# Cached scores of a hybrid decoder step: products on 64 rows by 32 columns, memory and small-branch scores in a PSUM bank of their own, and cache copies issued at other places

## Chip, cores and metric

The kernel runs on one core of one Trainium2 chip. The metric is the device time of one execution in microseconds, as a median of runs. All matrix data are float32.

## What is computed

One decoder layer serves 256 prompt tokens and, beside them, 8 sequences with 4 new tokens each ("sample" tokens, 32 in all) that have a past of 2,048 tokens. One projection gives queries, keys and values of three attention branches and gates; then come the branches, a merge, an output projection, and a mixture of 32 experts of which each token uses 4. The part that the change touches is the attention of the sample tokens over the cached keys:

```python
idx_a = la + jnp.arange(n_new)[:, None] - jnp.arange(SWA_WINDOW)[None, :]
oa, _ = gathered_attention(qa, ka_ext, va_ext, idx_a, sink)          # branch A: last 128, 2 kv heads, 8 query heads
ob = dilated_sample(qb, kb_ext, vb_ext, lb)                          # branch B: 4 kv heads, three dilations
oc = memory_attention(qc, cache_mem_k[l], cache_mem_v[l])            # branch C: 256 memory tokens, 4 heads
...
swa_k_s.append(ka_ext[:, n_new:])                                    # caches moved on by the 4 new rows
dil_k_s.append(kb_ext[:, n_new:])
```

The last two lines (and their like for the values) are pure copies: the dilated caches are 8 x 2 MB of keys and 8 x 2 MB of values that go from HBM to HBM.

## The kernel before

The program is written engine by engine, with semaphores and an order set out by hand. Its stages for this case:

- **Projection, 0 to 100 us.** Weight blocks of 512 columns (2 MB; block 4 only 256 columns) alternate between two buffers, `load_wblk(i)`. SP asks for block i when TensorE is done with block i - 2. Block 5 holds the memory weights, blocks 6 to 11 the gate weights, 12 and 13 the branch weights.
- **Prompt attention with gate products in between, 100 to 204 us** (`score_products` at L1238, `gate_products` at L1192).
- **Cached scores, 204 to 256 us.** For each cached sequence b, `load_cache(b)` brings some 1.2 MB of keys in six transfers; TensorE transposes them in 19 pieces (`k_transposes`, L1340), VectorE and ScalarE evict them to `kTs` (L466, L926), and TensorE multiplies the queries with them (L1356). The order on TensorE is transposes of b + 1, then scores of b. Three key buffers exist: the load of cache i waits for the transposes of cache i - 3. The query operand `qw` is zero outside the four columns of sequence b, which ScalarE fills (`window_queries`, L890), so that all eight sequences add up into the same PSUM rows.
- **Softmax of these scores under gate products, then values, 256 to 303 us** (VectorE L1977 to L1998; `PR_B`, `PR_C`, `PR_A` are the three branches in SBUF; L1422 and L1430 the value products).
- **Branch and output projections, routing, experts, 303 us to the end.** SP streams 2 MB pieces of the experts' weights through nine buffers (`load_pair`, L611).

In the scores each matmul contracts over all 128 rows and writes 32 PSUM rows. Head h = 2m + r has its queries in the 64 rows of half r of `qw[:, r]`; the other half of the rows is zero. Heads 0 to 3 go to the four groups of 32 columns of the array. The small branch A has 2 x 4 products of 128 columns, kept in two planes v. PSUM banks 0 to 3 hold, by columns, `SC_B` (0 to 1247), `SC_C` (1248 to 1503, bank 2) and `SC_A` (bank 3, with new keys).

SP's queue is one order of transfers. `copy_cache()` issues the next of the 16 copies. Before, one stands behind each of the weight blocks 2 to 8, then come the key loads 0 and 1, the stores of the new keys and values, three copies, block 9 with two copies, block 10 with two copies, block 11, key load 2, two small copies of the branch A caches (L589), and the other loads; two copies remain and stand behind the first two pieces of the experts' weights (309 us).

Of the kernel before, what the change touches and what calls it, by code (L numbers as in the profile page):

```python
# [16 lines left out]
ALU = mybir.AluOpType  # L17
# [35 lines left out]
def constants():  # L53

    cols, at = [], {}

    def put(name, a):
        a = np.asarray(a, np.float32).reshape(P, -1)
        at[name] = (sum(c.shape[1] for c in cols), a.shape[1])
        cols.append(a)  # L60

    p = np.arange(P)
    put("ident", np.eye(P))
    put("tri", (p[:, None] < p[None, :]))
# [12 lines left out]
    put("mask_b", np.stack([np.where((dist >= 0) & (dist <= w) & (dist % d == 0), 0, NEG)  # L77
                            for w, d in GROUPS], 1))

    b, i = p // NQ_S % NB_S, p % NQ_S  # L80
    new_b, new_i = np.arange(NS) // NQ_S, np.arange(NS) % NQ_S
    same = b[:, None] == new_b
    before = new_i <= i[:, None]
    itself = new_i == i[:, None]
    put("smask_a", np.where(np.concatenate([np.arange(LA) > i[:, None], same & before], 1), 0, NEG))
    recent = 1536 + np.arange(512)
    far = np.arange(384) // 4 * 16 + np.arange(384) % 4
    near = 1536 + np.arange(128) // 4 * 16 + np.arange(128) % 4
    q = PAST + i[:, None]
    put("smask_b", np.where(np.concatenate([  # L90
        ((q - recent) % 4 == 0) & (q - recent <= 512),
        ((q - np.concatenate([far, near])) % 16 == 0) & (q - np.concatenate([far, near]) <= 2048),
        q - recent[384:] <= 128,
        same & before, same & itself, same & itself], 1), 0, NEG))
    half = HD // 8
    inv = np.float32(500000.0) ** (-np.arange(half, dtype=np.float32) / np.float32(half))
    pos = np.stack([p, P + p, PAST + p % NQ_S], 1).astype(np.float32)
    ang = (pos[:, :, None] * inv.astype(np.float32)).astype(np.float32)
    put("cos", np.cos(ang))
    put("sin", np.sin(ang))  # L100

    row_h, row_b, row_i, tile = p % 32 // 8, p % 8 // 4, p % 4, p // 32
    put("omask_bc", (row_h[:, None, None] == np.arange(4)) & (row_b[:, None, None] == np.arange(2)[:, None]))
    put("omask_a", (row_b == tile // 2)[:, None] & ((tile % 2)[:, None] == np.arange(2)))
    put("osel", np.arange(NS) == (8 * np.arange(4)[:, None] + 4 * row_b[:, None, None] + row_i[:, None, None]))
    put("orow", np.concatenate([row_h[:, None] == np.arange(4), (tile < 3)[:, None], (tile == 3)[:, None]], 1))
    return np.ascontiguousarray(np.concatenate(cols, 1)), at

def lay_params(gain_rows, sinks, b_router, w_router):  # L110

    return np.ascontiguousarray(np.concatenate([
        gain_rows.reshape(3, KC, P).transpose(2, 0, 1).reshape(P, 3 * KC),
        np.broadcast_to(sinks.reshape(1, 8), (P, 8)),
        np.repeat(sinks.reshape(2, 4).T, NS, 0),
        np.broadcast_to(b_router.reshape(1, NE), (P, NE)),
        w_router.reshape(KC, P, NE).transpose(1, 0, 2).reshape(P, KC * NE),
        gain_rows[2].reshape(4, P, 2).transpose(1, 0, 2).reshape(P, KC)], 1), dtype=np.float32)
# [7 lines left out]
def build(nc, d):  # L126
    es = ExitStack()
    with es:
# [29 lines left out]
        def const(name, n=P):  # L158
            a, w = CONST_AT[name]
            return cst[0:n, a:a + w]  # L160
# [72 lines left out]
        def bank(i, n=1):  # L233
            return ps[:, i * 512:(i + n) * 512]
# [121 lines left out]

        SP = bank(0, 4)
        SC_B = SP[:, 0:NSM_B]
        SC_C = SP[:, NSM_B:NSM_B + LM]
        SC_A = SP[:, 1536:1536 + 2 * NSM_A].rearrange("p (v n) -> p v n", n=NSM_A)  # L360
        PR_B = s_probs[:, 0:NSM_B]
        PR_C = s_probs[:, NSM_B:NSM_B + LM]
        PR_A = s_probs[:, NSM_B + LM:NSM_B + LM + 2 * NSM_A].rearrange("p (v n) -> p v n", n=NSM_A)
# [106 lines left out]
        def _(sp):  # L470
# [6 lines left out]
            def load_wblk(i):  # L477
# [11 lines left out]
                elif i in W_BR:  # L489
# [4 lines left out]
                    sp.dma_start(dst[:, 4:6, :], d["w_br_b"][0].rearrange("(m p) n -> p m n", p=P)[:, :, n]).then_inc(s, 16)  # L494
                    sp.dma_start(dst[:, 6:8, :], d["w_br_c"][0].rearrange("(m p) n -> p m n", p=P)[:, :, n]).then_inc(s, 16)

            copies = [(x, b) for x in ("k", "v") for b in range(NB_S)]

            def copy_cache():
# [67 lines left out]
            sp.dma_start(cst[:, P:], d["consts"][:, P:]).then_inc(S["cst_in"], 16)  # L567
            for i in range(1, 9):
                load_wblk(i)
                if i >= 2:  # L570
                    copy_cache()
            sp.wait_ge(S["tr_evicted"], TR_H + TR_Q)
            load_cache(0)
            load_cache(1)
            store_new_kv()
            copy_cache()
            copy_cache()
            copy_cache()
            for i in (9, 10):
                load_wblk(i)  # L580
                copy_cache()
                copy_cache()
            load_wblk(11)
            load_cache(2)
# [4 lines left out]
                sp.dma_start(dst.rearrange("b (a n) -> b a n", a=16), src.rearrange("b (a n) -> b a n", a=16)) \  # L589
                    .then_inc(S["copy_dma"], 16)  # L590

            for i in range(3, 12):
                load_cache(i)
            load_wblk(12)
            for i in range(12, 16):
# [490 lines left out]
        def _(pe):  # L1086
# [257 lines left out]
            for b in range(NB_S):  # L1344
                if b + 1 < NB_S:
                    k_transposes(b + 1)
                kTs = kTs2[b % 2]
                done = 5 * (b + 1)
                pe.wait_ge(S["ktv_evicted"], (done + 1) // 2)
                pe.wait_ge(S["kta_evicted"], done // 2)  # L1350
                pe.wait_ge(S["qw_ready"], b + 1)
                win = slice(28 - 4 * b, 60 - 4 * b)
                first, last = b == 0, b == NB_S - 1

                def add(out, lhs, rhs, start):
                    return pe.matmul(out, lhs, rhs, start=start, stop=last, skip_group_check=True)  # L1356

                for part in range(5):
                    for h in range(4):
                        m, r = h // 2, h % 2  # L1360
                        row = slice(32 * h, 32 * h + 32)
                        kb = kTs[:, m * 1024:m * 1024 + 896]
                        q = qw[:, r]
                        if part == 0:
                            add(SP[row, 0:512], q[:, 6 + m, win], kb[:, 0:512], first)
                        elif part == 1:
                            add(SP[row, 512:896], q[:, 8 + m, win], kb[:, 512:896], first)
                        elif part == 2:
                            add(SP[row, 896:1024], q[:, 8 + m, win],
                                kb[:, 0:512].rearrange("p (a s) -> p a s", s=16)[:, :, 0:4], False)  # L1370
                        elif part == 3:
                            add(SP[row, 1024:1152], q[:, 4 + m, win], kb[:, 384:512], first)
                        else:
                            add(SP[row, NSM_B:NSM_B + LM], q[:, 10 + m, win],
                                kTs[:, 1920 + m * LM:1920 + (m + 1) * LM], False)
                for v in range(2):
                    for j in range(4):
                        ins = add(SC_A[32 * j:32 * j + 32, v, 0:LA], qw[:, v, j, win], kTs[:, 896:1024],
                                  first and v == 0)
                ins.then_inc(S["s_scores_b"], 1)  # L1380

            for g in range(3):
                for h in range(4):
# [2 lines left out]
                              kT_v[:, 1 + m, SEQ:TT], start=False, stop=True, skip_group_check=True)  # L1386
            for v in range(2):
                for j in range(4):
                    ins = pe.matmul(SC_A[32 * j:32 * j + 32, v, LA:NSM_A], qn[:, v, j, :], kT_v[:, 0, SEQ:TT],
                                    start=False, stop=True, skip_group_check=True)  # L1390
            ins.then_inc(S["s_scores_done"], 1)

# [60 lines left out]
                              start=(g == 0), stop=False, skip_group_check=True)  # L1453
            for v in range(2):
                for j in range(4):
                    ins = pe.matmul(bank(4)[32 * j:32 * j + 32, 64 * v:64 * v + 64], pT_n[:, 1 + v, 32 * j:32 * j + 32],
                                    kv[0:NS, 2, 384 + 64 * v:448 + 64 * v], start=False, stop=True, skip_group_check=True)
            ins.then_inc(S["s_tok_done"], 1)
            pe.wait_ge(S["s_tokb_evicted"], 1)
# [367 lines left out]
        def _(v):  # L1827
# [147 lines left out]
            v.wait_ge(S["s_scores_done"], 1)  # L1975
            nb, ncc, na = s_st[:, 0:1], s_st[:, 1:2], s_st[:, 2:4]
            link(v.tensor_tensor(PR_B, SC_B, const("smask_b"), ALU.add))  # L1977
            v.tensor_tensor(PR_A, SC_A, const("smask_a").unsqueeze(1).to_broadcast([P, 2, NSM_A]), ALU.add)
            v.tensor_reduce(nb, PR_B, AX.X, ALU.max, negate=True)
            link(v.tensor_reduce(ncc, SC_C, AX.X, ALU.max, negate=True))  # L1980
            link(v.tensor_reduce(na, PR_A, AX.X, ALU.max))
# [425 lines left out]
```

## Time and profile before

| | |
|---|---|
| median of 3 runs | 1313.25 us (1311.59 to 1314.88) |
| profiled execution | 1311.65 us, span 1309.8 us |
| busy share | TensorE 94%, VectorE 31%, ScalarE 19%, GpSimd 3% |
| chain that ended last | TensorE 64%, DMA 31% |
| L1340 (transposes of keys) | 152 records, 204.5 to 249.0 us |
| L1356 (scores) | 448 records, 209.3 to 255.7 us |

### The profile page before, as it was taken

What the parts mean: (1) busy time and instruction counts of PE and PEld (TensorE: products, weight loads), DVE (VectorE), ACT (ScalarE), POOL (GpSimd) and SP (SyncE); (2) the same over time, 40 slices, a digit from 0 to 9 for tenths busy, and PEclk for the clock granted to TensorE, in tenths of its full rate; (3) what the DMA queues carried; (4) which work ended last, traced back from release to release, by engine and by line L of the source; (5) the groups of instructions that cost most, each with busy time, mean ns of one, the idle gap of its engine ahead of it and who ended that gap; (6) DMA issues with size and microseconds to landing.
All of it is one profiled execution on the core that took longest, in us unless ns stands there. A gap on an engine that the chain in (4) does not pass through costs nothing.

```text
span 1309.8 us, 15220 instructions
## 1 busy us (share of the span) xinstructions
PE 1236.6 (94%) x6387; PEld 530.0 (40%) x6402; DVE 400.8 (31%) x908; ACT 245.3 (19%) x487; POOL 34.7 (3%) x47
## 2 busy tenths in 40 slices
PE   9999997999999999999999999889999999999996
PEld 4456675667553333333333333223333333333332
DVE  2244452314444232142231314222231313222233
ACT  3212443213111211112011111101011111101012
POOL 0000005000020000000000000000000000000000
PEclk9999998999999999999999999999999999999999
DMA  8686999689989999999999999999999999999994
GB/s 303 239 315 231 339 369 288 192 256 353 364 312 393 409 427 428 427 426 428 427 428 427 428 428 427 428 426 428 427 428 427 427 428 427 426 428 427 429 426 194
DMA packets 71673, 499.19 MB, mean 381 GB/s; under 512 B 5952, under 2 KB 29120, under 8 KB 45984
## 3 DMA queue, kind: packets, MB, share of 16 engines
q1 hardware_dynamic: 70752, 495.80, 93.3%
q0 software_dynamic: 848, 2.36, 0.6%
q8 instruction: 53, 0.87, 0.3%
q14 instruction: 20, 0.16, 0.0%
HBM read 495.29 MB, written 36.96 MB: 406 GB/s over the span
## 4 chain that ended last, share of the span: by engine, by line
PE 64%; DMA 31%; DVE 2%; issue 1%; ACT 1%; SPq 0%; DVEq 0%; ACTq 0%
DMA ring<-in_w_gate_up 20%; PE ps L1724 18%; PE ps L1763 12%; DMA late<-in_w_gate_up 9%; PE ps L1192 7%; PE ps L1108 5%; PE ps L1680 3%; PE ps L1624 3%; PE ps L1474 2%; PE ps L1487 2%; PE ps L1356 1%; PE ps L1340 1%; PE ps L1741 1%; PE ps L1643 1%; PE ps L1170 1%; DMA cq<-in_cache_mem_k 1%
## 5 line engine op out<-in xcount | busy, mean ns | idle before, releaser
L1724 PE MATMUL ps<-ring,cq 128*64 128x512 f32 x1376 | 313.9, 599 | 27.6 <-DMA ring<-in_w_gate_up 27.6
L1724 PEld LDWEIGHTS ps<-ring,cq 128*64 128x64 f32 x1376 | 93.9, 137 | 220.0 <-issue 161.8
L1763 PE MATMUL ps<-ring,cq 128*64 128x512 f32 x656 | 148.8, 595 | 0.0
L992 ACT ACTIVATE cq<-ps 128x512 f32<-128x512 f32 x32 | 19.1, 597 | 456.6 <-PE ps L1741 456.6
L1192 PE MATMUL ps<-arena,ring 128*128 128x288 f32 x384 | 102.3, 412 | 2.0 <-ACT ring L836 2.0
L2230 DVE TENSOR_REDUCE stat<-ps 128x1 f32<-128x288 f32 x15 | 6.9, 457 | 290.0 <-PE ps L1656 290.0
L1724 PE MATMUL ps<-cq 128*64 128x512 f32 x336 | 77.0, 595 | 5.0 <-DMA cq<-in_w_gate_up 5.0
L1192 PEld LDWEIGHTS ps<-arena,ring 128*128 128x128 f32 x384 | 69.6, 189 | 25.6 <-issue 4.9
L1763 PEld LDWEIGHTS ps<-ring,cq 128*64 128x64 f32 x656 | 45.4, 136 | 80.9 <-issue 76.4
L1108 PE MATMUL ps<-ring,arena 128*128 128x512 f32 (+3 forms) x240 | 72.3, 555 | 0.9 <-DMA ring<-in_w_in 0.9
L2258 DVE TENSOR_TENSOR x_tok<-x_tok,ps 64x512 f32<-64x512 f32 (+2 forms) x51 | 43.9, 860 | 73.2 <-PE ps L1680 67.8
L1006 ACT ACTIVATE cq<-ps 64x512 f32<-64x512 f32 x32 | 18.8, 589 | 230.2 <-PE ps L1763 230.2
L1624 PE MATMUL ps<-h_tok,cq 128*64 128x512 f32 x248 | 60.0, 604 | 0.0
L2131 DVE TENSOR_TENSOR cq<-ps,params 128x512 f32<-128x512 f32 x31 | 21.3, 686 | 110.7 <-PE ps L1643 110.7
L1108 PEld LDWEIGHTS ps<-ring,arena 128*128 128x128 f32 (+1 forms) x240 | 31.8, 163 | 37.9 <-issue 34.9
L1724 PE MATMUL ps<-late,cq 128*64 128x512 f32 x176 | 41.2, 601 | 5.7 <-DMA late<-in_w_gate_up 5.7
L1724 PEld LDWEIGHTS ps<-cq 128*64 128x64 f32 x336 | 23.3, 136 | 49.5 <-issue 37.8
L1763 PE MATMUL ps<-arena,cq 128*64 128x512 f32 x176 | 39.7, 592 | 0.7 <-issue 0.7
L1763 PE MATMUL ps<-late,cq 128*64 128x512 f32 x176 | 40.2, 598 | 0.0
L1680 PE MATMUL ps<-late,cq 128*32 128x512 bf16 (+1 forms) x180 | 39.7, 378 | 0.0
L1724 PE MATMUL ps<-arena,cq 128*64 128x512 f32 x160 | 36.3, 596 | 3.1 <-DMA arena<-in_w_gate_up 3.1
L2143 DVE TENSOR_TENSOR cq<-cq,ps 128x512 f32<-128x512 f32 x32 | 22.0, 687 | 42.3 <-ACT ps L988 41.7
(371 smaller groups left out, 1211.0 us busy)
## 6 DMA issues: line engine op xcount, KB each, us to landing
ring<-in_w_gate_up SPq DMA_DIRECT2D x86, 2048.0 KB, 37.9
ring<-in_w_down SPq DMA_DIRECT2D x40, 2048.0 KB, 38.8
cq<-in_w_gate_up SPq DMA_DIRECT2D x20, 2048.0 KB, 38.6
late<-in_w_gate_up SPq DMA_DIRECT2D x11, 2048.0 KB, 37.1
arena<-in_w_down SPq DMA_DIRECT2D x11, 2048.0 KB, 40.3
arena<-in_w_gate_up SPq DMA_DIRECT2D x10, 2048.0 KB, 36.9
late<-in_w_down SPq DMA_DIRECT2D x10, 2048.0 KB, 38.8
ring<-in_w_in SPq DMA_DIRECT2D x9, 2048.0 KB, 12.0
```

The source lines that it names most:

```text
L992: act_e.activation(xTe if isinstance(b, int) and b == NE - 1 else aTe, bank(4)[:, :].rearrange("p (q m) -> p q m", m=P), ACT.Copy).then_in ...
L1108: ins = pe.matmul(bank((n % 2) * 3 + t)[k_rows(t, k), 0:b - a], hT_v[:, k, TOK0[t]:TOK0[t] + NTOK[t]], wblk[n % 2][:, k, 0:b - a], **k_gro ...
L1192: ins = pe.matmul(bank(gate_bank(m))[:, 0:TT], wblk[(6 + m // 4) % 2][:, k, (m % 4) * P:(m % 4 + 1) * P], hT_v[:, k, :], start=(k == 0), s ...
L1474: ins = pe.matmul(bank(3 * (dt % 2) + br)[:, 0:TT], wblk[blk % 2][:, k, (dt % 4) * P:(dt % 4 + 1) * P], oT[:, k, :], start=(k == ks[0]), s ...
L1487: ins = pe.matmul(bank(wout_bank[t][n])[k_rows(t, k), :], hT_v[:, k, TOK0[t]:TOK0[t] + NTOK[t]], wo[n][:, k, :], **k_group(t, k))
L1624: pe.matmul(bank(6)[64 * h:64 * h + 64, :], sel[:, t, :], h_row[t][:, h * 512:(h + 1) * 512], start=(t == 0), stop=False, skip_group_check ...
L1680: ins = pe.matmul(out, slot_hot[:, tok], y_part[i][:, 512 * h:512 * h + 512], start=(i == 0), stop=(i == 2), skip_group_check=True)
L1724: ins = pe.matmul(bank(gu0 + u)[64 * h:64 * h + 64, :], xTe[:, k % 4, (k // 4) * 64:(k // 4) * 64 + 64], pair_buf[slot][:, a:a + 512], sta ...
L1763: ins = pe.matmul(bank(7 if last else 5)[64 * h:64 * h + 64, :], aT[:, kk % 4, (kk // 4) * 64:(kk // 4) * 64 + 64], pair_buf[slot][:, a:a ...
L2131: v.tensor_tensor(xTe4, xps, gain_x, ALU.mult).then_inc(S["xt_ready"], 1)
L2143: v.tensor_tensor(act, u_clip, bank(gu0), ALU.mult).then_inc(S["act_ready"], 1)
L2258: v.tensor_tensor(xs, xs, rows, ALU.add).then_inc(S["sc_added"], 1)
```

## The change

The scores' products contract over 64 rows instead of 128: each takes the row half r in which its head's queries lie. The dilated products of head h keep column group h. The products of memory and of branch A ("crossed") use the same row half and the other column group of the pair m, so they lie on parts of the array that the dilated products leave out. They are issued between the dilated ones, and they write bank 3 alone; the new keys of branch A go to bank 2. Masks, sinks and selectors are laid out for the new rows, and one mask addition on VectorE becomes two. In SP's queue the copies are issued by a table: 2, 2, 2, 1, 1, 3, 1 behind the weight blocks 2 to 8, none behind the stores of the new keys, one each behind blocks 9 and 10, one behind key load 7, and one remains for 309 us.

```diff
+            COPIES_BEHIND = (0, 0, 2, 2, 2, 1, 1, 3, 1, 1, 1)
             for i in range(1, 9):
                 load_wblk(i)
-                if i >= 2:
+                for _ in range(COPIES_BEHIND[i]):
                     copy_cache()
...
             store_new_kv()
-            copy_cache()
-            copy_cache()
-            copy_cache()
             for i in (9, 10):
                 load_wblk(i)
-                copy_cache()
                 copy_cache()
             load_wblk(11)
             load_cache(2)
...
-            for i in range(3, 12):
+            for i in range(3, 8):
+                load_cache(i)
+            copy_cache()
+            for i in range(8, 12):
                 load_cache(i)
...
-        SC_C = SP[:, NSM_B:NSM_B + LM]
-        SC_A = SP[:, 1536:1536 + 2 * NSM_A].rearrange("p (v n) -> p v n", n=NSM_A)
+        SC_C = SP[:, 1536:1536 + LM]
+        SC_A = SP[:, 1536 + LM:2048].rearrange("p (s n) -> p s n", n=LA)
+        SN_A = SP[:, NSM_B:NSM_B + 2 * NS].rearrange("p (s n) -> p s n", n=NS)
...
-                for part in range(5):
+                def add(out, r, chunk, rhs, start):
+                    half = slice(64 * r, 64 * r + 64)
+                    return pe.matmul(out, qw[half, r, chunk, win], rhs[half], start=start, stop=last, skip_group_check=True)
+
+                def crossed(part, h):
+                    m, r = h // 2, h % 2
+                    row = slice(32 * (2 * m + 1 - r), 32 * (2 * m + 1 - r) + 32)
+                    if part == 0:
+                        return add(SC_C[row, :], r, 10 + m, kTs[:, 1920 + m * LM:1920 + (m + 1) * LM], first)
+                    return add(SC_A[row, part - 1, :], r, 2 * m + part - 1, kTs[:, 896:1024], False)
+
+                for part in range(4):
                     for h in range(4):
...
                         if part == 0:
-                            add(SP[row, 0:512], q[:, 6 + m, win], kb[:, 0:512], first)
+                            own = add(SP[row, 0:512], r, 6 + m, kb[:, 0:512], first)
+                            crossed(0, h)
                         elif part == 1:
-                            add(SP[row, 512:896], q[:, 8 + m, win], kb[:, 512:896], first)
+                            crossed(1, h)
+                            own = add(SP[row, 512:896], r, 8 + m, kb[:, 512:896], first)
+                            crossed(2, h)
                         elif part == 2:
-                            add(SP[row, 896:1024], q[:, 8 + m, win],
-                                kb[:, 0:512].rearrange("p (a s) -> p a s", s=16)[:, :, 0:4], False)
-                        elif part == 3:
-                            add(SP[row, 1024:1152], q[:, 4 + m, win], kb[:, 384:512], first)
+                            own = add(SP[row, 896:1024], r, 8 + m,
+                                      kb[:, 0:512].rearrange("p (a s) -> p a s", s=16)[:, :, 0:4], False)
                         else:
-                            add(SP[row, NSM_B:NSM_B + LM], q[:, 10 + m, win],
-                                kTs[:, 1920 + m * LM:1920 + (m + 1) * LM], False)
-                for v in range(2):
-                    for j in range(4):
-                        ins = add(SC_A[32 * j:32 * j + 32, v, 0:LA], qw[:, v, j, win], kTs[:, 896:1024],
-                                  first and v == 0)
-                ins.then_inc(S["s_scores_b"], 1)
+                            own = add(SP[row, 1024:1152], r, 4 + m, kb[:, 384:512], first)
+                own.then_inc(S["s_scores_b"], 1)
...
-            v.tensor_tensor(PR_A, SC_A, const("smask_a").unsqueeze(1).to_broadcast([P, 2, NSM_A]), ALU.add)
+            mask_a = const("smask_a").unsqueeze(1)
+            v.tensor_tensor(PR_A[:, :, 0:LA], SC_A, mask_a[:, :, 0:LA].to_broadcast([P, 2, LA]), ALU.add)
+            v.tensor_tensor(PR_A[:, :, LA:], SN_A, mask_a[:, :, LA:].to_broadcast([P, 2, NS]), ALU.add)
```

The other edits of the diff (constants `omask_bc`, `omask_a`, `orow`, the sinks in `lay_params`, the row group g in the products of new keys and new values) move rows and add no instruction.

## Rows read from the trace of the kernel before

**Rows 1.** Windows: stretch; busy of PE, PEld, DVE, ACT, POOL; clock, DMA share, GB/s
```profile
222.98:230.78 7.80, 7.80 (x76) 5.65 (x77) 1.25 (x2) 1.79 (x3) 6.03 (x9) 0.66 0.96 273
...
378.40:1309.80 931.40, 874.10 (x4098) 299.57 (x4113) 258.85 (x573) 140.79 (x237) 0.00 (x0) 0.99 0.99 417
```

**Rows 2.** Chain that ended last, in order of time: start us, us, what
```profile
204.50 2.45 PE ps L1340 x19
...
222.98 4.32 PE ps L1340 x19
227.30 3.48 PE ps L1356 x56
...
241.50 2.37 PE ps L1340 x19
243.87 2.95 PE ps L1356 x56
...
249.28 2.99 PE ps L1356 x56
252.55 0.25 ACT ring L890
252.93 3.00 PE ps L1356 x54
256.33 11.87 PE ps L1192 x48
```

**Rows 3.** Waits, 200 to 262 us: who waited for what, total, times, longest
```profile
PE ps L1340 <- DMA cq<-in_cache_mem_k: 4.4, 1, 4.4
...
PE ps L1340 <- DMA ring<-in_cache_mem_k: 0.9, 1, 0.9
```

**Rows 4.** The same chain, 64-row products of the prompt's scores, two row halves
```profile
161.52 1.50 PE ps L1238 x12
```

**Rows 5.** Timeline: memory weights' first product, last softmax step; in brackets idle before
```profile
86.65 1.55 PE L1170 MATMUL ps<-ring 128*128 128x512 f32 x3 [0.60 <-DMA ring<-in_w_mem_kv]
...
266.61 0.48 DVE L1998 TENSOR_TENSOR ring<-ring,stat 128x320 f32<-128x320 f32 x1
```

**Rows 6.** Windows of the DMA engines, columns as in the first group
```profile
42.80:56.00 13.20, 13.20 (x31) 5.92 (x32) 2.73 (x4) 3.86 (x6) 0.00 (x0) 1.00 0.81 317
73.00:77.00 4.00, 4.00 (x22) 1.09 (x20) 0.00 (x0) 0.84 (x2) 0.00 (x0) 1.00 0.00 0
195.00:207.00 12.00, 10.35 (x86) 8.47 (x84) 2.57 (x4) 5.45 (x10) 2.96 (x6) 1.00 0.86 299
...
356.00:372.00 16.00, 16.00 (x102) 11.37 (x100) 8.96 (x28) 2.86 (x5) 7.33 (x5) 1.00 0.65 209
```

**Rows 7.** Timeline of SP's queue: start, us until the last is issued
```profile
77.03 0.37 SPq L485 DMA_DIRECT2D ring<-in_w_mem_kv  x1
...
123.43 0.37 SPq L488 DMA_DIRECT2D ring<-in_w_in  x1
...
151.58 11.29 SPq L506 DMA_DIRECT2D out_dil_v_s<-in_cache_dil_v  x2
...
196.33 6.25 SPq L531 DMA_DIRECT2D ring<-in_cache_dil_k  x3
...
206.97 0.37 SPq L528 DMA_DIRECT2D cq<-in_cache_dil_k  x1
```

**Rows 8.** DMA issues at 42, 76, 207, 227 us: KB, us to landing
```profile
ring<-in_w_in SPq DMA_DIRECT2D x1, 2048.0 KB, 7.8
...
ring<-in_w_mem_kv SPq DMA_DIRECT2D x1, 2048.0 KB, 9.6
...
cq<-in_cache_mem_k SPq DMA_DIRECT2D x1, 256.0 KB, 13.0
...
cq<-in_cache_mem_k SPq DMA_DIRECT2D x1, 256.0 KB, 4.1
```

**Rows 9.** Timeline of TensorE, value products of cache 0 and the first of cache 1
```profile
274.34 0.42 PE L1422 MATMUL ps<-cq,late 128*32 128x256 f32 x3 [0.72 <-ACT late L945]
...
275.67 0.41 PE L1422 MATMUL ps<-cq,late 128*32 128x256 f32 x2
```

More of the change, by code:

```diff
@@ L102, in constants @@
     row_h, row_b, row_i, tile = p % 32 // 8, p % 8 // 4, p % 4, p // 32
-    put("omask_bc", (row_h[:, None, None] == np.arange(4)) & (row_b[:, None, None] == np.arange(2)[:, None]))
-    put("omask_a", (row_b == tile // 2)[:, None] & ((tile % 2)[:, None] == np.arange(2)))
+    put("omask_bc", ((row_h ^ (tile == 3))[:, None, None] == np.arange(4)) & (row_b[:, None, None] == np.arange(2)[:, None]))
+    put("omask_a", (row_b == tile // 2)[:, None] & ((1 - row_h % 2)[:, None] == np.arange(2)))
     put("osel", np.arange(NS) == (8 * np.arange(4)[:, None] + 4 * row_b[:, None, None] + row_i[:, None, None]))
-    put("orow", np.concatenate([row_h[:, None] == np.arange(4), (tile < 3)[:, None], (tile == 3)[:, None]], 1))
+    put("orow", np.concatenate([(2 * (row_h // 2) + tile % 2)[:, None] == np.arange(4), (tile < 3)[:, None], (tile == 3)[:, None]], 1))
     return np.ascontiguousarray(np.concatenate(cols, 1)), at
@@ L114, in lay_params @@
         np.broadcast_to(sinks.reshape(1, 8), (P, 8)),
-        np.repeat(sinks.reshape(2, 4).T, NS, 0),
+        np.repeat(np.stack([sinks.reshape(2, 4)[1 - g % 2, 2 * (g // 2):2 * (g // 2) + 2] for g in range(4)]), NS, 0),
         np.broadcast_to(b_router.reshape(1, NE), (P, NE)),
@@ L1353, in _ @@
                 first, last = b == 0, b == NB_S - 1
-                def add(out, lhs, rhs, start):
-                    return pe.matmul(out, lhs, rhs, start=start, stop=last, skip_group_check=True)
-                for part in range(5):
+                def add(out, r, chunk, rhs, start):
[8 more added lines that the diff above has]
+                for part in range(4):
                     for h in range(4):
@@ L1362, in _ @@
                         kb = kTs[:, m * 1024:m * 1024 + 896]
-                        q = qw[:, r]
                         if part == 0:
-                            add(SP[row, 0:512], q[:, 6 + m, win], kb[:, 0:512], first)
+                            own = add(SP[row, 0:512], r, 6 + m, kb[:, 0:512], first)
+                            crossed(0, h)
                         elif part == 1:
-                            add(SP[row, 512:896], q[:, 8 + m, win], kb[:, 512:896], first)
+                            crossed(1, h)
+                            own = add(SP[row, 512:896], r, 8 + m, kb[:, 512:896], first)
+                            crossed(2, h)
                         elif part == 2:
-                            add(SP[row, 896:1024], q[:, 8 + m, win],
-                                kb[:, 0:512].rearrange("p (a s) -> p a s", s=16)[:, :, 0:4], False)
-                        elif part == 3:
-                            add(SP[row, 1024:1152], q[:, 4 + m, win], kb[:, 384:512], first)
-                        else:
-                            add(SP[row, NSM_B:NSM_B + LM], q[:, 10 + m, win],
-                                kTs[:, 1920 + m * LM:1920 + (m + 1) * LM], False)
-                for v in range(2):
-                    for j in range(4):
-                        ins = add(SC_A[32 * j:32 * j + 32, v, 0:LA], qw[:, v, j, win], kTs[:, 896:1024],
-                                  first and v == 0)
-                ins.then_inc(S["s_scores_b"], 1)
+                            own = add(SP[row, 896:1024], r, 8 + m,
+                                      kb[:, 0:512].rearrange("p (a s) -> p a s", s=16)[:, :, 0:4], False)
+                        else:
+                            own = add(SP[row, 1024:1152], r, 4 + m, kb[:, 384:512], first)
+                own.then_inc(S["s_scores_b"], 1)
             for g in range(3):
@@ L1388, in _ @@
                 for j in range(4):
-                    ins = pe.matmul(SC_A[32 * j:32 * j + 32, v, LA:NSM_A], qn[:, v, j, :], kT_v[:, 0, SEQ:TT],
+                    g = 2 * (j // 2) + 1 - v
+                    ins = pe.matmul(SN_A[32 * g:32 * g + 32, j % 2, :], qn[:, v, j, :], kT_v[:, 0, SEQ:TT],
                                     start=False, stop=True, skip_group_check=True)
@@ L1455, in _ @@
                 for j in range(4):
-                    ins = pe.matmul(bank(4)[32 * j:32 * j + 32, 64 * v:64 * v + 64], pT_n[:, 1 + v, 32 * j:32 * j + 32],
+                    g = 2 * (j // 2) + 1 - v
+                    ins = pe.matmul(bank(4)[32 * j:32 * j + 32, 64 * v:64 * v + 64], pT_n[:, 1 + j % 2, 32 * g:32 * g + 32],
                                     kv[0:NS, 2, 384 + 64 * v:448 + 64 * v], start=False, stop=True, skip_group_check=True)
```

## The prediction

> **What bounds the kernel now.** I read the page's chain first, then the windows, the chain in order of time, the waits and the DMA views of 195 to 256 us. From 378 us on the experts' weights keep the DMA engines full (share 0.99 for 931 us) [rows 1]; this stretch starts when the work before it ends, so what is saved ahead of it moves the end by as much. Before 378 us TensorE works almost without a pause, except where the cached scores are made, from 204.5 us (end of the wait for L883) to the first gate product at 256.33. Its chain is: transposes of a cache (T, L1340), scores of the cache before (S, L1356), eight of each. Undisturbed T takes 2.37 to 2.45 us (2.42) and S 2.95. Eight of each are 43.0 us, 0.66 goes to the wait for the last query window (252.27 to 252.93), 0.40 to the new keys behind the last S, so 44.1 [rows 2]. The stage lasts 51.8. The rest is waiting for keys: 0.9 for cache 2, 4.4 for cache 3 [rows 3]; after that the granted clock of the stretch is 0.66 [rows 1], so the engine fell to its 1.2 GHz level for part of it, and T and S beside it take 4.32 and 3.48 [rows 2], 1.9 and 0.5 above the later ones. Together 7.7 us lost to late keys. So two terms are in reach: 8 S, and 7.7.
>
> **Change, part 1: the scores.** A float32 matmul is two records here. 48 records of 288 columns take 11.87 us [rows 2]: 0.86 ns a column and record, 1.72 ns a column of a matmul. Before, each of four column groups takes 512 + 384 + 128 + 128 (dilated) + 256 (memory) + 2 x 128 (small branch) = 1,664 columns: 2.86 us, against 2.95 measured, so the four groups do run beside each other and almost nothing else counts. The diff contracts over 64 rows, not 128, and puts memory and small branch on the other row half in the other column group of the pair. Still 28 matmuls, 56 records; a group's dilated products are 1,152 columns, 1.98 us, and its 512 others should run beside them. That two row halves overlap the trace shows at L1238: six matmuls of 64 rows and 256 columns would be 2.64 us in a line and 1.32 in two, and take 1.50 [rows 4]. That is 0.18 above the columns. No row shows two row halves together with four column groups. Bounds for S: 1.98 below, 2.95 above where the halves don't overlap (the same columns in a line), exclusion is a rival. I take 1.98 + 0.18, and 0.04 for eight streams to start instead of two, 2.2, by the L1238 row, which is the same kind of pair. Saved: 8 x 0.75 = 6.0 us (bounds 7.8 and 0).
>
> Can the transposes keep pace? The evictions of T end during the S behind it: with 0.69 us each on VectorE the last ends about 0.7 us after T, still inside 2.2. The 0.66 for the last window stays.
>
> On VectorE the mask add of 128x320 (0.48 us at that size) becomes two, 128x256 and 128x64: an estimate of 0.15 us more, the fixed part of one such step, from the same size at L1998. The last normalising step ends at 267.09 and TensorE comes out of its gate products at 268.20 [rows 2, 5]: slack of about 1 us, so nothing; without that cover 0.15. The new keys keep 40 records; masks, sinks and selectors change only in values.
>
> **Change, part 2: the copies.** 16 copies of 2 MB, HBM to HBM, stand in SP's queue. Before, 7 are issued behind weight blocks 2 to 8, 3 behind the stores of new keys, 4 behind blocks 9 and 10, 2 at 309 us. After: 12 behind blocks 2 to 8 (2, 2, 2, 1, 1, 3, 1), 2 behind 9 and 10, 1 behind key load 7, 1 at 309. A load with a copy moved 13.2 us x 317 GB/s = 4.2 MB in the stretch 42.8 to 56 with a share of 0.81, so 10.7 us for both; 5.3 for a copy.
>
> Early on this is hidden. The engines are empty at 73 to 77 (share 0.00) [rows 6]. Load 2 with two copies is 16 us from 28, to 44; load 3 the same to about 60, its block landed long before that (7.8 us with a copy behind it [rows 8]); block 4 is half as large, with two copies to about 75.5; the memory weights are asked for at 77.03. They already come 0.6 us late (9.6 us from issue, TensorE free at 86.05) [rows 5, 7, 8], so a copy still moving there counts at once: 0 taken, bounds 0 and 2. Behind block 7, from 101 us, load and three copies are 21 us, and block 8 is asked for at 123.43 [rows 7]. SP's own issues (0.6 us each, 11.3 for two where the ring is full [rows 7]) delay only SP waits that are for TensorE anyway.
>
> Between 144 and 195 us five copies fewer, 26 us of transfers: no wait for a transfer stands there, so nothing there, but the backlog at 195 goes. Of 26.9 MB issued from 123 to 195 windows of 2 us show 25.8 moved, so about 1.1 MB was left, 3 to 4 us at the 299 GB/s of 195 to 207 [rows 6]. And SP was held 6.25 us in issuing load 2's far keys [rows 7]. A cache is 1.25 MB, 4.6 us at the 273 GB/s that the engines give while they carry keys (share 0.96) [rows 1]. After: block 11 (5 us), keys 2 (4.6), the small copies (2.5), biases (1.5) from 196.5 on end at 210; keys 3, asked for at 206.97, at 214.7 by bytes alone, against 222.9 (its last piece took 13.0 us; unloaded 4.1 [rows 8]). The faster TensorE now wants them at 204.5 + 3 x 2.42 + 2 x 2.2 = 216.1. Then it wants one cache every 4.6 us, which is what a cache takes. So keys and TensorE bound the stage about equally up to cache 7, and the copy behind load 7 (about 227 us) runs against that load's own last pieces. I leave 1.5 us of stalls and a full clock: 7.7 - 1.5 = 6.2 saved (bounds 7.7 and, if keys 3 to 7 land no earlier, about 0 with half of term 1 lost too).
>
> The copy taken from 309: share 0.65 at 356 to 372 [rows 6], the engines idle because all nine weight buffers are full; nothing, bound 5.3.
>
> **Sum.** 6.0 + 6.2 = 12.2 us, the stage ends at 244.1. Profiled: 1311.65 us (span 1309.8) to 1299.4. The median is 1313.25, 1.6 above that execution: 1301.0.
>
> **Rivals.**
> 1. Keys still decide. If keys 3 land at 223 as before, T of cache 3 starts there and its slow clock stays; only the five S behind it gain, 3.8 to 4.5: 1309. For it: the chain's 13 us for one 256 KB piece, three loads in flight, which get in each other's way. Against: 1.1 MB less ahead of them, and SP not held at 196.
> 2. Issue order costs. At L1422/L1430 the products of the next cache start at 275.67 on column groups whose own four records, 0.22 apart from 274.34, ended at about 275.2 [rows 9]: a full group holds up the others. If each group holds only one matmul ahead, the crossed 128-column ones, issued before the own ones, push heads 2 and 3 back by 0.2 to 0.4 us: S 2.5, 2.4 us less gain: 1303.5.
> 3. The row halves run no closer than before: S 2.95, only 6.2: 1307.
> 4. Slower: the two row halves exclude each other while four column groups are in use, at the own products of heads 0 and 1, which write one PSUM bank from different halves. Heads alternate between the halves in the program, so each waits for the last: 4 x 1.98 = 7.9 us, the stage ends at 204.5 + 19.4 + 1.1 + 8 x 7.9 = 288.2, 31.9 later: 1345. It decides from S = 3.9 us, where the stage ends at 256.3 again. Against: L1238 shows halves overlapping, though in different banks.
> 5. A copy makes the memory weights late, 2 to 5 us: 1304 to 1306.
> 6. The copy taken from 309 helps after all, up to 5.3: 1296.
>
> Beside rival 4, the Trainium skill, TensorEngine Tiling (Array Packing), Gotcha 1, says that different row tiles can't write one PSUM bank at the same time; the diff gives a bank of its own only to memory and small branch. No row here shows that case. By that rule it would be the exclusion; heads 0 and 1 write different partitions, which is why I hold it small.
>
> Beside rival 2, the Trainium skill, TensorE: Matmul & The Clock Gate, step-by-step part, says that matmuls stay in program order and only weight loads are pulled ahead. By that rule, taken strictly, S before would be about 5.7 us (each of 6,656 columns for one record); by that rule the trace does not agree, with 2.95.
>
> **How the numbers follow.** Forecast 0.60; rival 1 0.12; 2 0.10; 3 0.06; 4 0.04; 5 0.04; 6 0.04. Range 1296.5 to 1308.5: both terms at their best (15.5 us, 1297.7) and the spread of the three runs below, rivals 2, 3 and 5 above; half of rival 1 and all of 4 stay out. The forecast's own range is 1298 to 1303. A measurement tells about 0.3%, 3.9 us, from no change. Faster 0.87 (all but 4 and part of 1), same 0.09, slower 0.04.
>
> **What would show it.** S at L1356 near 2.2 us (forms of 64 rows), first gate product behind it near 244; no wait above 2 us for keys 2 or 3 and a granted clock of 1.00 throughout 204 to 244; the wait for memory weights at 86 us still 0.6; DMA share near 1 from 196 to 235; the stretch from 378 us (then 366) as long as before, 931. Wrong if S is above 2.6, if T of cache 3 starts after 219, if the copy behind load 7 makes cache 7 late by more than 2 us, or if the last stretch changes its length.

## The result, and the profile after

The changed kernel takes 1303.62 us (median of 6 runs, 1302.45 to 1306.16), the kernel before 1312.26 us in the 6 runs beside it: ratio 0.9935, 95% interval 0.9924 to 0.9945, 8.6 us faster. The forecast was 1301.0 in a range of 1296.5 to 1308.5. Two more sets on other occasions gave 1301.53 against 1312.53 (0.9928, 0.9903 to 0.9953) and 1303.80 against 1311.87 (0.9934, 0.9921 to 0.9948): 11.0 and 8.1 us faster. The profiled execution took 1302.55 us with a span of 1300.7.

The chain that ended last, in order of time, answers to [rows 2] (start us, us, what; L1341 are the transposes, L1358 the scores, L1193 the gate products):

```profile
78.82 10.54 DMA ring<-in_w_mem_kv
89.41 14.00 PE ps L1171 x32
...
207.26 2.45 PE ps L1341 x19
...
212.71 6.43 DMA cq<-in_cache_mem_k
219.18 2.53 PE ps L1341 x19
221.71 2.52 PE ps L1358 x40
224.23 2.37 PE ps L1341 x19
226.60 2.29 PE ps L1358 x40
228.89 2.46 PE ps L1341 x19
231.35 2.29 PE ps L1358 x40
...
243.81 2.33 PE ps L1358 x40
...
246.68 11.87 PE ps L1193 x48
```

From the first transposes to the first gate product the stage is 246.68 - 207.26 = 39.4 us, against 51.8. S is 2.29 us instead of 2.95 (the chain counts 40 of its 56 records, the timeline has all). The chain still passes through the transfer of keys 3 (L1341 at 219.18), but this is no wait any more: its last piece lands 6.4 us after issue, not 13.0 [rows 8], hardly later than TensorE gets there. The waits of TensorE up to 262 us, against [rows 3]:

```profile
PE ps L1109 <- DMA ring<-in_w_in: 2.2, 2, 1.5
...
PE ps L1171 <- DMA ring<-in_w_mem_kv: 1.6, 1, 1.6
...
PE ps L1358 <- ACT ring L891: 0.7, 1, 0.7
```

No wait for keys is among the eight largest (the smallest of those is 0.5 us); of the loads, only those of the first weight block and the memory weights are left, and both are longer than before (0.9 and 0.6 then). The windows (stretch; busy of PE, PEld, DVE, ACT, POOL; clock, DMA share, GB/s), against [rows 1]:

```profile
207.26:246.68 39.42, 38.65 (x641) 31.24 (x641) 13.29 (x20) 14.91 (x34) 21.08 (x30) 1.00 1.02 328
246.68:1300.70 1054.02, 999.18 (x4894) 380.07 (x4893) 310.32 (x705) 166.66 (x289) 9.32 (x9) 0.99 0.97 402
```

In the stage the clock is 1.00 and the DMA engines are full at the same time (1.02): both bounds are met at once. The stretch behind it is 1054.0 us, 0.5 longer than before (1309.8 - 256.33 = 1053.5). The 12.4 us of the stage shrink to 9.1 in the span because this execution was late on the way: the piece of the first weight block that SP asks for at 3.1 us landed at 13.06 us instead of 11.27, ahead of the first copy (1.8 us), the memory weights took 1.0 us more from issue to landing than before, and 0.5 us came in behind the stage. So everything between 89 and 207 us stands 2.76 us later than before.

### The profile page after: what moved, and what is told of

Read it like the earlier page. It is cut to its first block, busy times and chain, and to the rows that moved or that the text cites. A ratio compares the mean times of both kernels' runs of the same rounds, so it can differ in the third digit from the quotient of the medians.

```text
span 1300.7 us, 15236 instructions
## 1 busy us (share of the span) xinstructions
PE 1234.3 (95%) x6402; PEld 530.1 (41%) x6402; DVE 403.4 (31%) x909; ACT 245.3 (19%) x487; POOL 34.7 (3%) x47
## 4 chain that ended last, share of the span: by engine, by line
PE 60%; DMA 36%; DVE 2%; ACT 1%; issue 1%; SPq 0%; DVEq 0%; ACTq 0%
DMA ring<-in_w_gate_up 19%; PE ps L1730 17%; PE ps L1769 11%; DMA cq<-in_w_gate_up 9%; PE ps L1193 7%; PE ps L1109 5%; DMA late<-in_w_gate_up 3%; DMA ring<-in_w_down 3%; PE ps L1630 3%; PE ps L1480 2%; PE ps L1493 2%; PE ps L1341 1%; PE ps L1649 1%; PE ps L1686 1%; PE ps L1358 1%; PE ps L1171 1%
## 5 line engine op out<-in xcount | busy, mean ns | idle before, releaser
L1193 PE MATMUL ps<-arena,ring 128*128 128x288 f32 x384 | 102.3, 412 | 2.1 <-ACT ring L837 2.1
L1193 PEld LDWEIGHTS ps<-arena,ring 128*128 128x128 f32 x384 | 69.6, 189 | 25.6 <-issue 4.9
L1007 ACT ACTIVATE cq<-ps 64x512 f32<-64x512 f32 x32 | 18.9, 591 | 230.5 <-PE ps L1769 230.5
L1769 PE MATMUL ps<-late,cq 128*64 128x512 f32 x176 | 40.2, 598 | 0.0
```

Of the source, the lines that this page charges most:

```text
L1193: ins = pe.matmul(bank(gate_bank(m))[:, 0:TT], wblk[(6 + m // 4) % 2][:, k, (m % 4) * P:(m % 4 + 1) * P], hT_v[:, k, :], start=(k == 0), s ...
L1769: ins = pe.matmul(bank(7 if last else 5)[64 * h:64 * h + 64, :], aT[:, kk % 4, (kk // 4) * 64:(kk // 4) * 64 + 64], pair_buf[slot][:, a:a ...
```

## The experiments

Stage below means the time from the first transposes of keys to the first gate product behind the scores, read from each chain. The profile of each is of one execution.

**The two parts by themselves.** `scores_only` keeps the new products and issues the copies at the old places; `copies_only` is the reverse.

```diff
 # scores_only, against the changed kernel
-            COPIES_BEHIND = (0, 0, 2, 2, 2, 1, 1, 3, 1, 1, 1)
+            COPIES_BEHIND = (0, 0, 1, 1, 1, 1, 1, 1, 1, 2, 2)
...
             store_new_kv()
+            copy_cache()
+            copy_cache()
+            copy_cache()
             for i in (9, 10):
                 load_wblk(i)
+                copy_cache()
                 copy_cache()
...
-            for i in range(3, 8):
-                load_cache(i)
-            copy_cache()
-            for i in range(8, 12):
+            for i in range(3, 12):
                 load_cache(i)
```

> The scores' products as changed, the copies at their old places. If late keys set the first half of the stage whatever the products take, S falls to 2.3 us, the transposes of cache 3 still begin some 18 us after those of cache 0, at a low clock after the wait, and only the five S behind them gain: 3.3 to 4 us, 1308 to 1309. If keys were late only because copies were ahead of them by chance and the shorter S counts eight times, 5.3 us: 1307. In both cases the wait for the memory weights stays 0.6.

> The copies at their new places, the scores' products as before. If the copies alone made the keys late, no wait above 1 us stands in the stage, the clock is 1.00 throughout, S stays 2.95 and the stage falls from 51.8 to 44.5; less 1.0 for memory weights that come later: 6.3 us, 1306. If the three loads in flight get in each other's way whatever is ahead, a wait of 3 us or more for keys 3 stays and the gain is under 3 us.

scores_only: 1308.01 us against 1312.53, ratio 0.9965 (0.9952 to 0.9977). Its chain:

```profile
203.81 2.45 PE ps L1342 x19
...
210.52 12.12 DMA cq<-in_cache_mem_k
222.68 3.72 PE ps L1342 x19
226.40 2.49 PE ps L1359 x40
228.89 2.37 PE ps L1342 x19
231.25 2.29 PE ps L1359 x40
```

Its waits for keys:

```profile
PE ps L1342 <- DMA cq<-in_cache_mem_k: 3.4, 1, 3.4
...
PE ps L1342 <- DMA ring<-in_cache_mem_k: 2.0, 1, 2.0
```

The last piece of keys 3 again takes 12.1 us, its transposes begin 18.9 us after those of cache 0 (18.5 before), and take 3.72 us: what the first scores save is waited away, and the stretch 216 to 228 has a clock of 0.84 here too. The stage is 251.24 - 203.81 = 47.4 us, 4.4 less than before: 0.4 above the first reading's 3.3 to 4, and short of the second's 5.3. The wait for the memory weights was 0.5 us.

copies_only: 1305.62 us, ratio 0.9956 (0.9938 to 0.9974). Its chain:

```profile
205.48 4.91 PE ps L1340 x38
210.40 2.95 PE ps L1356 x56
213.34 2.37 PE ps L1340 x19
215.71 2.95 PE ps L1356 x56
218.66 2.46 PE ps L1340 x19
...
249.61 11.87 PE ps L1192 x48
```

Transposes and scores follow each other without a gap: 44.1 us, 7.7 less, exactly what the late keys and the slow clock had cost. Here, too, three loads of keys are in flight, so it was the copies' places that made the keys late. The memory weights cost 0.1 us more than before (a wait of 0.7), not the 1.0 that was taken off, and the kernel gained 6.9 us, not 6.3. The two parts add up: 4.4 + 7.7 = 12.1, against 12.4, 11.7 and 11.7 in three executions of both (`changed_again` 245.54 - 205.46 = 40.1, `changed_third` 248.06 - 207.95 = 40.1). If the keys are already in time, the scores save 44.1 - 39.4 to 40.1, 4.0 to 4.7 us, of 5.3, since 0.6 to 1.3 us come back as waits.

**The changed kernel again, and the start.**

> The changed kernel once more beside the others: 8 to 9 us under the kernel before. If the 1.8 us by which its first weights came later is chance between executions, the start of the products of pair 4 to 5 of block 0 moves again, by a microsecond or so either way; if it belongs to the change, it stands near 13.1 us again and near 11.3 in the kernels with the old copies.

> The changed kernel on the same chip as the run before it: 8.5 to 11 us under the kernel before, the memory weights 1.6 to 2.1 us late, and 1 to 2 us above the kernel with the copies taken from behind blocks 3 and 4.

The gains of these two sets, 11.0 and 8.1 us, lie outside what was expected of them (8 to 9, and 8.5 to 11). The same piece of the first weight block landed at 10.74 and 11.88 us, against 13.06 in the first profile; the kernel before has 11.27, scores_only 10.69, copies_only 12.12. The start moves by up to 2.4 us between executions, of one kernel and from kernel to kernel, before anything of the change is issued; it is no effect of it. TensorE waited 2.1 and 1.8 us for the memory weights.

**Who makes the memory weights late.** `copy_off_block4` has the table 2, 2, 1, 1, 2, 3, 1 behind blocks 2 to 8, `mem_clear` 2, 1, 1, 1, 2, 3, 2, `mem_clear_309` 2, 1, 1, 1, 2, 3, 3 with none left for 309 us. Only the tuple differs from the changed kernel.

```diff
-            COPIES_BEHIND = (0, 0, 2, 2, 2, 1, 1, 3, 1, 1, 1)
+            COPIES_BEHIND = (0, 0, 2, 2, 1, 1, 2, 3, 1, 1, 1)    # copy_off_block4
+            COPIES_BEHIND = (0, 0, 2, 1, 1, 1, 2, 3, 2, 1, 1)    # mem_clear
+            COPIES_BEHIND = (0, 0, 2, 1, 1, 1, 2, 3, 3, 1, 1)    # mem_clear_309
```

> The changed kernel with one copy taken from behind block 4 and put behind block 6 (table 2, 2, 1, 1, 2, 3, 1). If the second copy behind block 4 makes the memory weights late, the engines are empty again just ahead of their issue, TensorE waits 0.6 us for them instead of 1.6, and the whole is 1 us faster than the changed kernel. If the later weights come from the later start of that execution, the wait stays at 1.6 and nothing moves.

> The changed kernel with table 2, 1, 1, 1, 2, 3, 2: one copy each behind blocks 3 and 4, as in the kernel before, two behind 6 and 8. The run with one copy off block 4 had empty engines ahead of the memory weights and TensorE still waited 1.6 us. If copies in the two blocks ahead make these weights late in some way other than a queue, the wait falls to 0.6 here and the kernel is 1 us faster than the changed one. If the 0.6 to 2.1 us are chance from one execution to the next, it lies anywhere between and the times are the same within 1 us.

> The table 2, 1, 1, 1, 2, 3, 3: one copy each behind blocks 3 and 4 and none left for 309 us. The wait for the memory weights is 0.6 us. If the experts' stream starts only when its nine buffers are full and the engines idle ahead of it, the stretch from the first gate product behind the scores to the end stays 1053.5 to 1055 us and the kernel is 1 to 2 us faster than the changed one, by the memory weights alone. If the copy at 309 us delays the stream, that stretch is up to 5 us shorter.

The wait, from the waits of copy_off_block4, and the engines ahead of the issue (columns as above):

```profile
PE ps L1171 <- DMA ring<-in_w_mem_kv: 1.6, 1, 1.6
```

```profile
72.00:78.00 6.00, 6.00 (x27) 2.03 (x25) 0.00 (x0) 0.84 (x2) 0.00 (x0) 1.00 0.03 11
```

With one copy off block 4 the engines are empty (share 0.03, 0.97 in the changed kernel), and the weights are as late as ever. The other way round, in copies_only the share ahead of the issue is 0.89 and the wait 0.7. The later start of the execution is not the reason either: changed_again started early (10.74 us) and waited 2.1, mem_clear late (12.48) and waited 0.6. With one copy each behind blocks 3 and 4, mem_clear has:

```profile
PE ps L1171 <- DMA ring<-in_w_mem_kv: 0.6, 1, 0.6
```

Over all kernels, one profile each: with one copy behind each of blocks 3 and 4, the wait was 0.6, 0.5, 0.6 and 0.5 (before, scores_only, mem_clear, mem_clear_309). With more it was 1.5 to 2.2 in eight executions and 0.7 in two (copies_only, copies_at_gates). copies_at_gates has the same copies as copy_off_block4 up to block 5, and waited 0.7 against 1.6, so chance between executions has a part. That the copies behind blocks 3 and 4 have another, of about 1 us, is what the fourteen waits suggest; it is not shown. A queue that hasn't drained at 78 us isn't the explanation, and how an earlier copy could delay a load when the engines have run empty in between stays open.

The late weights can cost more than their wait. In changed_third, copy_off_block4 and copies_at_stores (waits of 1.8, 1.6, 1.6 us) the 32 products behind them took 15.6 to 15.7 us instead of 14.0; in the other five executions with a wait of 1.5 us or more, changed_again among them, they took 14.0. Chain and windows 84 to 104 of changed_third:

```profile
88.48 15.63 PE ps L1171 x32
```

```profile
84.00:104.00 20.00, 18.19 (x59) 8.33 (x58) 11.53 (x41) 1.58 (x3) 0.00 (x0) 0.91 0.87 348
```

and of changed_again:

```profile
84.00:104.00 20.00, 17.93 (x68) 9.27 (x61) 12.90 (x44) 1.77 (x4) 0.00 (x0) 1.00 0.80 304
```

The granted clock fell in one and not in the other, though the other's wait was longer (2.1 us).

copy_off_block4 took 1301.03 us against 1312.53, ratio 0.9913 (0.9896 to 0.9930), the lowest of all the sets, although its profile has the late weights and the slow clock; that profile is of its slowest execution (1304.28, the others 1300.3 to 1301.2). mem_clear took 1301.58 us against 1311.03, ratio 0.9928 (0.9914 to 0.9942). mem_clear_309 took 1301.53 against 1311.87, 0.9922 (0.9909 to 0.9934), on the chip where changed_third took 1303.80, 0.9934. Both beat the kernel before; over the changed kernel the 2.3 us (1 to 2 were expected) are of the size that the wait and the clock explain, but the intervals overlap, and copy_off_block4 is as fast, so a gain from this is not shown. The stretch behind the stage was 1299.7 - 244.60 = 1055.1 us with no copy at 309 us, no shorter than with one: that copy delays nothing.

**Issue order, and what is beside what.** `crossed_last` issues the crossed products behind all dilated ones; `own_only` leaves out the crossed products of caches 1 to 7.

```diff
 # crossed_last: the calls of crossed() in the parts are gone, and instead
+                for part in range(3):
+                    for h in range(4):
+                        own = crossed(part, h)
                 own.then_inc(S["s_scores_b"], 1)
...
 # own_only, at each of the three calls
-                            crossed(0, h)
+                            if b == 0:
+                                crossed(0, h)
```

> The changed kernel with the crossed products issued behind all dilated ones of a cache, the same 28 matmuls. If a part of the array that holds four records holds up all that is issued behind it, the crossed ones start only when the last dilated ones are let in, at 1.5 to 1.6 us, and S is 2.6 to 2.7 us. If a part holds only two, 2.9 or more. If issue order doesn't matter, S stays 2.29.

> Leaves out the memory and small-branch scores of caches 1 to 7 (their softmax runs on the scores of cache 0 alone). What is left are 16 matmuls a cache, 1,152 columns in each column group. If the crossed products are fully beside the dilated ones, S falls only from 2.29 to some 2.15 us (1.98 of columns and 0.18), and the rest of the gap to 1.98 belongs to filling and draining. If the two row halves share something that slows both, S falls to 2.05 or less.

One T and S late in the stage, crossed_last:

```profile
238.10 2.46 PE ps L1341 x19
240.56 2.60 PE ps L1358 x48
```

and own_only:

```profile
235.09 2.08 PE ps L1358 x32
237.17 2.46 PE ps L1341 x19
```

crossed_last has S 2.56 to 2.63, 0.27 or more above the changed order, at or a little under the 2.6 to 2.7 of the reading with four records held for each part; so issue order counts, and the reading with two held (2.9 or more) doesn't fit. The weight loads of crossed_last agree (timeline of PEld, in brackets the idle time before): the dilated products have 32 of the 56; the first 20 come in fours and an eight, at the pace of the products, and the last 12 and all 24 crossed ones from 232.08 on.

```profile
230.55 0.15 PEld L1358 LDWEIGHTS ps<-ring 64*32 64x32 f32 x8 [0.17 <-issue]
231.01 0.13 PEld L1358 LDWEIGHTS ps<-ring 64*32 64x32 f32 x4 [0.30 <-issue]
231.44 0.13 PEld L1358 LDWEIGHTS ps<-ring 64*32 64x32 f32 x4 [0.30 <-issue]
231.76 0.13 PEld L1358 LDWEIGHTS ps<-ring 64*32 64x32 f32 x4 [0.20 <-issue]
232.08 0.83 PEld L1358 LDWEIGHTS ps<-ring 64*32 64x32 f32 x36 [0.20 <-issue]
```

In own_only S is 2.08: 1,152 columns at 1.72 ns are 1.98, and 0.10 is all that filling and draining add, as before the change (0.09). So the 512 crossed columns cost 0.21 us of the 0.88 that they would cost in line: three quarters of that time is hidden, not all. The value lies between the two that were expected, at 2.15 and at 2.05, so it doesn't tell whether the 0.21 is issue (twelve more matmuls between the starts of the dilated ones) or something that the halves share.

**Which copies hold up the keys.** Seven copies stand between 144 and 195 us before, two in the changed kernel. `copies_at_stores` has five there (three behind the stores, one each behind blocks 9 and 10, table 1, 2, 1, 1, 1, 2, 1 for blocks 2 to 8), `copies_at_gates` four (two each behind 9 and 10, table 2, 2, 1, 1, 1, 2, 1). `copy7_late` leaves the copy behind key load 7 to 309 us.

```diff
-            COPIES_BEHIND = (0, 0, 2, 2, 2, 1, 1, 3, 1, 1, 1)
+            COPIES_BEHIND = (0, 0, 1, 2, 1, 1, 1, 2, 1, 1, 1)    # copies_at_stores
...
             store_new_kv()
+            copy_cache()
+            copy_cache()
+            copy_cache()
...
+            COPIES_BEHIND = (0, 0, 2, 2, 1, 1, 1, 2, 1, 2, 2)    # copies_at_gates
...
                 load_wblk(i)
+                copy_cache()
                 copy_cache()
...
             for i in range(3, 8):                                # copy7_late
                 load_cache(i)
-            copy_cache()
```

> The changed kernel with three copies put back behind the stores of new keys (145 us), one behind each of blocks 9 and 10, and nine behind blocks 2 to 8. If only the backlog that is left at 195 us makes the keys late, the engines work these three off by 190, no wait above 1.5 us for keys stands in the stage, and it lasts 39.4 to 40.1 us as in the changed kernel. If the number of copies between 144 and 195 us counts, waits of 2 to 5 us come back.

> The changed kernel with two copies each behind blocks 9 and 10 as before, none behind the stores, ten behind blocks 2 to 8. If what is asked for last before 195 us makes the backlog, keys 3 are late again by 1.5 to 4 us. If it takes all seven copies of the kernel before to overfill the engines (26 us more), the two extra ones, 10.6 us, find room and no wait above 1.3 us stands in the stage.

> The changed kernel with the copy behind key load 7 left to 309 us, two there as before. If that copy ran against the last keys, the small stretch between the transposes of cache 4 and cache 7 shortens by a few tenths; if it is hidden, the stage stays 39.4 to 40.1 us. The stretch behind the scores stays 1053.5 to 1055 in both cases if the copies at 309 us are hidden.

The waits for keys are 1.0 us in copies_at_stores, 0.3 in copies_at_gates, 1.0 in copy7_late (up to 1.3 in the others with both parts); the stages 40.2, 39.4 and 40.0 us. So five copies in these 50 us cost at most a few tenths and seven cost 7.7 us. The windows say where the difference lies: the DMA engines of copies_at_stores stand empty for 9 us before block 11 is asked for (at 198.92), and so do those of copies_at_gates (share 0.03 at 190 to 195); those of the kernel before are full up to that point (block 11 at 195.29). First copies_at_stores, then the kernel before:

```profile
190.00:199.00 9.00, 8.72 (x44) 6.31 (x43) 4.30 (x8) 4.96 (x21) 0.00 (x0) 1.00 0.00 0
```

```profile
186.00:195.00 9.00, 8.72 (x42) 6.34 (x41) 4.27 (x10) 5.09 (x20) 0.00 (x0) 1.00 1.18 456
```

By an estimate from these 9 us and the 5.3 us of a copy, a sixth copy would still be free and a seventh not; no run has six. So it is not a price for each copy, and the windows speak for a threshold: the copies are free until the engines can no longer clear their queue before block 11 is asked for. crossed_last, own_only and these three kernels ran once each (1302.45, 1301.68, 1305.24, 1300.89 and 1302.32 us), so their stages are compared and not their times.

The copy behind key load 7 is hidden, and the stretch behind the stage is 1054.2 us with two copies at 309.

## Why the prediction was right

- **What bounds the kernel: right.** The stage's end moved and everything behind it kept its length: 1053.5 us before, 1053.6 to 1055.1 in the thirteen other profiles (0.1 to 1.6 us longer, with and without the change's parts). The gain was where the forecast put it, in the stage: 12.4, 11.7 and 11.7 us, against 12.2.
- **Scores, 6.0 us: mechanism right, size a tenth too large.** The row halves do run beside each other under four column groups. S came out at 2.29, not 2.2; 8 x 0.66 = 5.3 us. The 0.04 for eight streams was too little: the crossed products take 0.21, while the 0.18 from L1238 was too much (0.10). Rival 3 (S 2.95) is out with it.
- **Rival 4** is out: own_only has heads 0 and 1 write one bank from different row halves in 2.08 us. The rule of the Trainium skill, TensorEngine Tiling (Array Packing), Gotcha 1, that was put beside it is not followed here as far as partitions differ.
- **Rival 2** has its mechanism (crossed_last, 0.27 us a cache), but the diff's interleaving avoids at least that much; whether the 0.21 that is left is issue stays open. The rule of the Trainium skill, TensorE: Matmul & The Clock Gate, in its step-by-step part, that matmuls stay in program order, does not fit if it is read as one matmul after another: with both records 6,656 columns would be 11.4 us (the 5.7 of the prediction counts one record), against S of 2.95 before. Read as the order of their starts, it is not contradicted: crossed_last agrees that what is issued later waits behind what is issued earlier.
- **Late keys, 6.2 us: right.** Alone, the copies brought all 7.7. Beside the faster S they brought 7.1 in the first profile and 6.4 in the other two, with waits for keys of up to 1.1 us, of 1.5 allowed. That this is a little more than forecast and the scores a little less evens out in the sum, and that is luck. Rival 1 did not come: it is what scores_only shows, 1308.0 where it was priced at 1309.
- **Where the backlog comes from: partly wrong.** The sum of bytes gave 3 to 4 us of backlog and keys 3 at 214.7. They landed at 219.14, which is 216.4 on the clock of the kernel before (less the 2.76 us by which this execution was late): 1.7 us later than by bytes alone, why is open, and just what the faster TensorE wants. The sign "T of cache 3 starts after 219" was met at 219.18 only through that late start. The backlog was also told as an amount, where the runs show a threshold between five and seven copies.
- **Early copies, 0: the step that failed.** "0 taken, bounds 0 and 2": the memory weights were 1.6 to 2.1 us late instead of 0.6 in the changed kernel's three profiles, and the clock fell behind it in one. That is 1.0 to 1.5 us, and 2.8 where the clock fell (1.2 and 1.6), outside the bounds. Rival 5, with a chance of 0.04 and a price of 2 to 5 us, is nearer to it. The reason given, a copy still moving at 77 us, doesn't hold, since the weights are as late behind empty engines; whether the early copies are the cause at all is suggested and not shown.
- **VectorE's second addition, 0: right.** The two are 0.42 and 0.21 us; the last step ends at 257.5 with the gate products running to 258.56.
- **Copy at 309, 0: right**, shown by mem_clear_309. Rival 6 is out.

Sum for the profiled execution: 5.3 + 7.1 = 12.4 in the stage, less 1.0 for the memory weights, 1.8 for a late start that is chance and 0.5 behind the stage: 9.1 measured in the span. The same sum for changed_again is 11.7, plus 0.5 for an early start, less 1.5 for the memory weights and 0.3 behind the stage, 10.5 measured; for changed_third 11.7, less 0.6 for the start, 1.2 for the memory weights, 1.6 for the clock and 0.6 behind the stage, 7.7 measured.

The number flatters the forecast. The gain was to be 12.2 us and was 8.6 (11.0 and 8.1 in the other sets). The median lies 2.6 us above 1301.0 and not 3.6 because the kernel before was 1.0 us faster in its six runs than in the three that the forecast started from; that is luck too. The three sums show where the microseconds went in three executions; for the medians they are not shown.

## What to carry to other kernels

When some operands use half of the array's rows, give the zero half to other products, in the other column group and another bank, and issue them between the long ones: here 512 columns beside 1,152 cost a quarter of their length. Background copies were free here as long as the DMA engines ran empty ahead of the next urgent load (five in 50 us), and with seven, where they didn't, cost 7.7 us with the slow clock behind the wait: look for that idle stretch, and place them by it and not evenly. And watch a load that is already a little late: a wait of 1.6 us is small, but in three of eight executions the clock fell behind one of its kind and doubled the loss.

## What was not expected of the hardware

- Two row halves write one PSUM bank at the same time, in different partitions, at no cost that shows (S 2.08 us for 1,152 columns).
- A 2 MB load asked for behind engines that were just empty took 10.6 us (copy_off_block4, share 0.03 ahead of it) or 9.6 (mem_clear). The kernels with more copies 16 to 34 us earlier have the longer time in eight profiles of ten, the others in none of four; in copies_only it took 9.7 us with a share of 0.89 ahead of it. The cause is open.
- A wait of 1.5 to 2.2 us for a load ended with a clock of 1.00 in some executions and with 0.91 over the next 20 us in others (1.6 us more for 32 products), with no order by the length of the wait.
